# Two transformer blocks on one core: the second block's first modulation as row sums on VectorE

## What is computed

```python
def _modulation(cvec, w_ada, b_ada):
    m = jax.nn.silu(cvec) @ w_ada + b_ada
    return jnp.split(m, 3, axis=-1)
...
    sh, sc, gt = _modulation(c, w_ada, b_ada)
    sh_c, sc_c, gt_c = _modulation(c_ctx, w_ada, b_ada)
    h = _rms(x, norm_w) * (1.0 + sc[:, None, :]) + sh[:, None, :]
    hc = _rms(xc, norm_w) * (1.0 + sc_c) + sh_c
...
def swiglu(x, w1, w3, w2):
    return (jax.nn.silu(x @ w1) * (x @ w3)) @ w2
```

## Time and profile before

| | |
|---|---|
| time of three runs | 1367.22 us median, 1361.17 to 1367.77 |
| span of the profiled execution | 1363.3 us (its own time is not given) |
| TensorE busy | 1344.2 us, 99% |
| VectorE busy | 790.6 us, 58% |
| ScalarE busy | 640.8 us, 47% |
| granted TensorE clock | full in all 40 slices |
| DMA | 215.43 MB, 158 GB/s over the span |

### The profile page before, as it was taken

How to read it: one execution, slowest core, us unless ns; L and a number is a source line. 1 busy time by engine, 2 the same in 40 slices (tenths; PEclk the granted TensorE clock), 3 DMA queues, 4 the chain that set the end, 5 groups by cost and what they waited for, 6 DMA issues and landing times.

```text
span 1363.3 us, 24540 instructions
## 1 busy us (share of the span) xinstructions
PE 1344.2 (99%) x10306; PEld 1200.5 (88%) x10306; DVE 790.6 (58%) x1239; ACT 640.8 (47%) x1126; POOL 160.1 (12%) x131
## 2 busy tenths in 40 slices
PE   9999999999999999999999999999999999999999
PEld 8989999999855899999987777888888888879999
DVE  6976666557767666655724567433333455775554
ACT  6645444444365554455433445323232345555442
POOL 0020111001300012110004000111011100301110
PEclk9999999999999999999999999999999999999999
DMA  8535767556597455665432210222222234414553
GB/s 319 186 124 185 229 226 256 188 186 217 186 336 267 150 190 191 199 197 173 140 115 94 93 56 32 93 93 93 93 93 95 92 122 144 147 61 153 194 186 124
DMA packets 60974, 215.43 MB, mean 158 GB/s; under 512 B 6720, under 2 KB 12736, under 8 KB 57408
## 3 DMA queue, kind: packets, MB, share of 16 engines
q1 hardware_dynamic: 56272, 206.59, 45.4%
q10 hardware_dynamic: 4592, 7.26, 1.5%
HBM read 208.59 MB, written 1.05 MB: 154 GB/s over the span
## 4 chain that ended last, share of the span: by engine, by line
PE 88%; DVE 7%; ACT 3%; issue 1%; DMA 1%; SPq 0%; POOL 0%; ACTq 0%; DVEq 0%; POOLq 0%
PE psum L329 24%; PE psum L330 23%; PE psum L331 23%; DVE WL L261 3%; PE psum L1246 3%; PE psum L1271 2%; PE psum L1409 2%; PE psum L326 1%; PE psum L327 1%; PE psum L328 1%; ACT WH L256 1%; PE psum L2714 1%; PE psum L1602 1%; DMA stage<-ab_in 1%; PE psum L1250 1%
## 5 line engine op out<-in xcount | busy, mean ns | idle before, releaser
L329 PE MATMUL psum<-XX,WH 128*128 128x256 f32 (+1 forms) x1912 | 584.7, 306 | 8.2 <-DVE WL L261 2.8
L331 PE MATMUL psum<-XX,WL 128*128 128x256 f32 (+1 forms) x1912 | 576.3, 301 | 0.0
L330 PE MATMUL psum<-XX,WH 128*128 128x256 f32 (+1 forms) x1912 | 576.3, 301 | 0.0
L261 DVE TENSOR_TENSOR WL<-stage,WH 128x1024 fp32r<-128x1024 f32 x332 | 397.1, 1236 | 254.9 <-ACT WH L256 254.7
L256 ACT ACTIVATE WH<-stage 128x1024 fp32r<-128x1024 f32 x332 | 333.4, 1052 | 330.1 <-PE psum L331 286.0
L329 PEld LDWEIGHTS psum<-XX,WH 128*128 128x128 f32 x1912 | 359.4, 188 | 39.7 <-issue 13.8
L331 PEld LDWEIGHTS psum<-XX,WL 128*128 128x128 f32 x1912 | 359.9, 188 | 15.9
L330 PEld LDWEIGHTS psum<-XX,WH 128*128 128x128 f32 x1912 | 358.8, 188 | 15.7 <-issue 0.5
L329 PE MATMUL psum<-hidden,WH 128*128 128x256 f32 x352 | 97.5, 277 | 0.0
L331 PE MATMUL psum<-hidden,WL 128*128 128x256 f32 x352 | 97.2, 276 | 0.0
L330 PE MATMUL psum<-hidden,WH 128*128 128x256 f32 x352 | 97.2, 276 | 0.0
(11 more groups left out here) (288 smaller groups left out, 1675.7 us busy)
## 6 DMA issues: line engine op xcount, KB each, us to landing
stage<-w SPq DMA_DIRECT2D x132, 512.0 KB, 4.6
stage<-merge SPq DMA_DIRECT2D x80, 512.0 KB, 4.5
ring<-ada SPq DMA_DIRECT2D x24, 1024.0 KB, 7.0
stage<-in SPq DMA_DIRECT2D x44, 512.0 KB, 4.5
stage<-ab_in SPq DMA_DIRECT2D x22, 512.0 KB, 5.8
stage<-nsa_in SPq DMA_DIRECT2D x20, 512.0 KB, 4.8
stage<-out SPq DMA_DIRECT2D x16, 512.0 KB, 4.2
stage<-ab_out SPq DMA_DIRECT2D x8, 512.0 KB, 4.7
```

Source lines behind the costliest of these rows:

```text
L261: e.tensor_tensor(lo, raw, hi.bitcast(F32), ALU.subtract).then_inc(s_lo, 1)
L329: e.matmul(dst, wh, xh, start=start, stop=False)
L330: e.matmul(dst, wh, xl, start=False, stop=False)
L331: return e.matmul(dst, wl, xh, start=False, stop=stop)
```

## The change

The first layer's modulation leaves TensorE. Its matrix is laid out transposed: 24 rows of 128 features, each feature in one partition with its 1024 weights along the row. `cvecs` holds both vectors, copied into every partition. ScalarE takes the SiLU of them once in each feed-forward layer. `modulation_row` multiplies a row of weights with each vector and sums along it, so two instructions give 128 features for both vectors. Fourteen rows stand in f0 (c = 1 to 10 and m = 1 to 4), ten in f1 (c = 1 to 10). Their weights take twelve ring slots, which SyncE loads between the stage loads. The second layer's twelve blocks stay in the attention, spread over its 27 steps. The diff, cut to its core:

```diff
--- before.py
+++ after.py
+        ROWS = list(range(1, 8)) + list(range(21, 26))
...
         def ring_load(e, rings, name, src):
             if n >= NSLOT:
-                e.wait_ge(*pe.of(f"ring{n - NSLOT}"))
+                e.wait_ge(*(ve if n - NSLOT in ROWS else pe).of(f"ring{n - NSLOT}"))
...
         def ring_take(e, rings, cols, shape, **dims):
+            while rings.n in ROWS:
+                rings.n += 1
...
@@ ffn_vector, up-projections
                 if c > 0:
                     low_next(e, flow)
+                    modulation_row(e, l, 14 * l + c - 1)
                 e.wait_ge(*pe.of(f"{p}.w3.{c}"))
@@ ffn_vector, down-projections
+                if l == 0 and 1 <= m <= 4:
+                    modulation_row(e, l, 9 + m)
                 e.wait_ge(*pe.of(f"{p}.w2.{m}"))
@@ ffn_scalar
                 if c == 0:
                     inverse_scalar(e, p)
+                    meet(e, *["hn"[l] + ".end"] * 4)
+                    e.dma_start(M.rows, A["cvecs"].rearrange("p (v n) -> p v n", v=2)).then_inc(s_rows, 16)
                 e.wait_ge(*ve.of(f"{p}.up.{c}"))
                 e.activation(F.sg[c % 3], F.sg[c % 3], ACT.Silu).then_inc(*ac.tick(f"{p}.silu{c}"))
+                if c == 0:
+                    e.wait_ge(s_rows, 16 + 16 * l)
+                    e.activation(M.rows, M.rows, ACT.Silu).then_inc(*ac.tick(f"m.rows{l}"))
@@ ffn_sync
             for c in range(22 + 11):
                 load_next(e, flow)
-                if c in (12, 16, 20):
-                    next(ahead, None)
+                if c in ((0, 1, 2, 9, 13, 17, 21, 25, 29, 31), (0, 1, 2, 9, 13))[l]:
+                    next(ahead)
@@ new
+        M.rows, M.spent = view(2048, 2048, **two), C("decay", 768, 1024)
+
+        def modulation_row(e, l, t):
+
+            n = ROWS[t // 2]
+            w = ring[:, n % NSLOT * SLOT + t % 2 * 1024:n % NSLOT * SLOT + t % 2 * 1024 + 1024]
+            e.wait_ge(*ac.of(f"m.rows{l}"))
+            e.wait_ge(s_slot[n % NSLOT], 16 * (n // NSLOT + 1))
+            for v in range(2):
+                if v == 0 and t > 0:
+                    e.wait_ge(*ve.of(f"m.row{t - 1}"))
+                e.scalar_tensor_tensor(out=(M.spent, w)[v], in0=w, scalar=1.0, in1=M.rows[:, v, :], op0=ALU.mult, op1=ALU.mult,
+                                       accum_out=MODS[0][:, t, v:v + 1]).then_inc(*ve.tick(f"m.row{t}"))
+            if t % 2 == 1:
+                ve.mark(f"ring{n}")
+            if t == 23:
+                modulation_ends(e, 0)
+
+        def modulation_ends(e, l):
+
+            bias, nw = [v.rearrange("p (m a) -> p m a", a=1).to_broadcast([128, n, 2])
+                        for v, n in ((P("b_ada", 24 * l, 24), 24), (P("norm_w2", 8 * l, 8), 8))]
+            e.wait_ge(*ve.now())
+            e.tensor_tensor(MODS[l], MODS[l], bias, ALU.add).then_inc(*ve.tick())
+            e.wait_ge(*ve.now())
+            e.scalar_tensor_tensor(out=MODS[l][:, 8:16, :], in0=MODS[l][:, 8:16, :], scalar=1.0, in1=nw, op0=ALU.add,
+                                   op1=ALU.mult).then_inc(*ve.tick(f"m.{l}"))
@@ modulation_tensor, _turns, _vector, _scalar
-            for c in range(24):
+            for c in range(12):
@@ nsa_tensor, nsa_vector, nsa_scalar
-            attend_tensor(e, "n", N.units, N.S, N.T, scores, values, beside, evenly(24, 24), last, turns)
+            attend_tensor(e, "n", N.units, N.S, N.T, scores, values, beside, evenly(24, 10), last, turns)
@@ nsa_ahead, final_ahead, nsa_sync
+            for j in range(7):
+                ring_load(e, rings, f"rows{j}", A["ada_0"][j])
+                yield
-            for name, src in (("cmp_1", A["cmp_1"]), ("ada0", A["ada"][0]), ("ada1", A["ada"][1])):
+            for name, src in (("cmp_1", A["cmp_1"]), ("ada0", A["ada_1"][0]), ("ada1", A["ada_1"][1])):
...
+        def final_ahead(e, rings):
+            for j in range(7, 12):
+                ring_load(e, rings, f"rows{j}", A["ada_0"][j])
+                yield
...
-            for c in range(2, 24):
-                ring_load(e, rings, f"ada{c}", A["ada"][c])
+            for c in range(2, 12):
+                ring_load(e, rings, f"ada{c}", A["ada_1"][c])
@@ the arrays
-    arr["ada"] = np.ascontiguousarray(I["w_ada_2"].reshape(2, 4, 2, 128, 3, 4, 256).transpose(0, 4, 1, 3, 5, 2, 6)).reshape(
-        24, 128, 2048)
+    arr["ada_0"] = np.ascontiguousarray(I["w_ada_2"][0].T.reshape(12, 2, 128, 1024).transpose(0, 2, 1, 3)).reshape(12, 128, 2048)
+    arr["ada_1"] = np.ascontiguousarray(I["w_ada_2"][1].reshape(4, 2, 128, 3, 4, 256).transpose(3, 0, 2, 4, 1, 5)).reshape(
+        12, 128, 2048)
+    arr["cvecs"] = np.ascontiguousarray(np.broadcast_to(np.concatenate([I["c_2"][0], I["c_ctx_2"]])[None], (128, 2048)))
```

More of the change, by code:

```diff
@@ L178, in build @@
         s_out = sem("out_landed")
+        s_rows = sem("vector_rows_landed")
         s_swap = {name: sem(f"swapped_{name}") for name in SWAPPED}
@@ L1181, in ffn_scalar @@
                     square_scalar(e, "fn", m)
+                    if m == 0:
+                        e.wait_ge(*ve.of("m.0"))
                     e.activation(SQ1[:, m, :], X[:, m, NOW], ACT.Square, scale=P("final_norm", m)).then_inc(
@@ L1200, in ffn_gpsimd, with ffn_sync @@
             gp.mark(f"{p}.end")
-        def ffn_sync(e, flow, l, ahead=()):
-            ahead = iter(ahead)
+        def ffn_sync(e, flow, l, ahead):
             for c in range(22 + 11):
                 load_next(e, flow)
-                if c in (12, 16, 20):
-                    next(ahead, None)
+                if c in ((0, 1, 2, 9, 13, 17, 21, 25, 29, 31), (0, 1, 2, 9, 13))[l]:
+                    next(ahead)
                 if l == 0 and c == 8:
@@ L1426, in modulation_vector @@
         def modulation_vector(e):
-            for c in range(24):
+            for c in range(12):
                 if c % 4 == 3:
                     u = c // 4
-                    l, m = u // 3, u % 3 * 8
-                    to = MODS[l][:, m:m + 8, :].rearrange("p (g j) v -> p j g v", j=2)
-                    bias = P("b_ada", 24 * l + m, 8).rearrange("p (g j a) -> p j g a", j=2, a=1).to_broadcast([128, 2, 4, 2])
+                    m = u * 8
+                    to = MODS[1][:, m:m + 8, :].rearrange("p (g j) v -> p j g v", j=2)
+                    bias = P("b_ada", 24 + m, 8).rearrange("p (g j a) -> p j g a", j=2, a=1).to_broadcast([128, 2, 4, 2])
                     e.wait_ge(*pe.of(f"m.v{u}"))
@@ L1436, in modulation_vector @@
                     banks.emptied(f"m.v{u}", ve)
-                    if u % 3 == 2:
-                        nw = P("norm_w2", 8 * l, 8).rearrange("p (m a) -> p m a", a=1).to_broadcast([128, 8, 2])
+                    if u == 2:
+                        nw = P("norm_w2", 8, 8).rearrange("p (m a) -> p m a", a=1).to_broadcast([128, 8, 2])
                         e.wait_ge(*ve.now())
-                        e.scalar_tensor_tensor(out=MODS[l][:, 8:16, :], in0=MODS[l][:, 8:16, :], scalar=1.0, in1=nw,
-                                               op0=ALU.add, op1=ALU.mult).then_inc(*ve.tick(f"m.{l}"))
+                        e.scalar_tensor_tensor(out=MODS[1][:, 8:16, :], in0=MODS[1][:, 8:16, :], scalar=1.0, in1=nw,
+                                               op0=ALU.add, op1=ALU.mult).then_inc(*ve.tick("m.1"))
                 yield
         def modulation_scalar(e):
-            for c in range(24):
+            for c in range(12):
                 if c % 4 == 3:
@@ L1732, in finish @@
                     banks.emptied(f"n.value{it}{t2}{f}", ve)
-            attend_vector(e, "n", N.units, N.S, N.T, finish, beside, evenly(24, 24), True)
+            attend_vector(e, "n", N.units, N.S, N.T, finish, beside, evenly(24, 10), True)
             residual_vector(e, flow, "n", "f1", "n.begun")
@@ L1790, in done @@
                     e.activation(N.part(XH, n), N.value(n), ACT.Copy).then_inc(*ac.tick(f"n.xh{n}"))
-            attend_scalar(e, "n", N.units, N.S, N.T, beside, evenly(24, 24), True, done)
+            attend_scalar(e, "n", N.units, N.S, N.T, beside, evenly(24, 10), True, done)
             residual_scalar(e, flow, "n", "f1", ((ve, 23),))
@@ L2950, in sync @@
             nsa_sync(e, flow, rings)
-            ffn_sync(e, flow, 1)
+            ffn_sync(e, flow, 1, final_ahead(e, rings))
             layer_sync(e, flow, rings, 0)
```

## The result

The changed kernel takes 1374.08 us (median of 9 runs), the kernel before 1366.79 beside it (9 runs). The ratio is 1.0078, with an interval of 1.0057 to 1.0098: some 11 us slower by the ratio, 7.3 by the medians, where 1366.4 and no measurable change was forecast. The profiled executions have spans of 1371.9 and 1363.3 us, 8.6 apart. Between these two it is the same, so their stages may be subtracted.

What follows compares the result with a forecast made beforehand. TensorE was taken to bound the kernel, at 88% of the chain. Attention -11.6, down-projections +3.2 and transfer waits +7.6 sum to -0.8 us on the median 1367.2, giving 1366.4; range 1358 to 1378, likeliest case 1361 to 1373.

Steps and rivals of the forecast that it cites:

- ScalarE's wait for the transfer: Both feed-forward stages: ScalarE stands until both vectors land, delaying w3's second high parts; +4.2 and +3.4, together 7.6 us.
- I take 7.0: Feed-forward stages: assumed landing time in us of the 1 MB transfer, between 5.3 and 9.0 seen for others.
- the prediction's own rule: First turns of both stages: landing time passes into the wait; 5.3 us takes 1.7 off each, 9.0 adds 2.0.
- Rival B: Feed-forward stages: ScalarE's wait for the transfer decides; landings of 11 us give +7.2, 1374 us; chance 0.15.
- The attention: Sparse attention: removing twelve modulation blocks and three transpose pairs saves 7.6 us in the second half, 4.0 in the first.
- a group lasts from 427.50 to 439.66, 12.16 us: Attention's second half: a group of three units falls from 12.16 to 10.25 us, saving 1.9 each, 7.6 for four.
- Down-projections: First layer, m = 1 to 4: rows ahead of the residual delay ScalarE's high parts; +3.2 us, 2.0 with rows of 2.4.
- Up-projections: Both feed-forward layers: a row brings VectorE to 9.65 of a 10.88 us turn, so it fits; 0 us.
- The bound of 4.0 us: Up-projections: row time on VectorE up to which the added row still fits in a turn.
- Rival C: VectorE's product with a sum runs at half pace, slowing up- and down-projections; +24 us, 1391 us; chance 0.1.

Runs made afterwards that it cites:

- experiment 2: Three variants of the changed kernel: ring loads at chunks 0, 3, 6; at 4, 5, 6; transfer and products cut to two columns: ratios 1.0075, 1.0092, 1.0013.
- experiment 3: Changed kernel plus 12 extra fp32 products on TensorE ahead of the second w3 chunk in both layers: ratio 1.0049.
- experiment 5: Changed kernel with the SiLU one turn later, and the attention's twelve modulation blocks multiplying 16 of 256 columns: ratio 0.9921.
- experiment 4: Changed kernel with the SiLU one turn later, and the first layer's down-projection row products behind the residual and its low part: ratio 0.9949, measured again 0.9925.
- experiment 7: Changed kernel with the SiLU one turn later, and GpSimd's gate multiplication over 2 of 256 columns: span 1361.8 us, first products 1.22 us.
- the kernel with the loads apart: Changed kernel with each layer's second and third ring loads issued at chunks 3 and 6, not 1 and 2: ratio 1.0075.
- the fastest version: Changed kernel with SiLU one turn later, down-projection rows behind the residual, and five extra products in the attention's step 1: ratio 0.9919, span 1350.1 us.

## Why the prediction was wrong, step by step

- **ScalarE's wait for the transfer**: the right place and mechanism, the term mis-sized. It had 4.2 + 3.4 = 7.6 and measured 7.6 + 7.15 = 14.8. Of the 7.2 missing, two steps. The first is "I take 7.0" for the landing. That is what it takes with no ring load near it (6.8 and 7.4, experiment 2), and there the holes are 3.7 and 3.6, near the 4.2 and 3.4 reckoned. With the three loads it was 8.4 and 9.3, for which the prediction's own rule gives 5.6 and 5.7 (measured 5.3 and 5.5). That is 3.3. The other 3.9 has no step at all in the prediction, which forecast the holes but put nothing behind them: the granted clock was at 0.50 there, and it costs about 1.8 us each (experiment 3). Nothing in the profile before could show it, since its clock is full everywhere and it has no hole of 5 us.
- **Rival B** named this wait, but put the point from which it decides at a landing of 11 us. With the clock's part it decided at 8.4 and 9.3.
- **The attention**: -11.6 forecast, -9.0 measured. The failed step is "a group lasts from 427.50 to 439.66, 12.16 us": that was one group, taken for all four. TensorE's timeline of the kernel before has the scores that open the two groups ahead of it at

```profile
406.82 1.13 PE L1246 MATMUL psum<-arena 64*128 64x256 f32 x8
...
417.12 1.14 PE L1246 MATMUL psum<-arena 64*128 64x256 f32 x8
```

so these took 10.3 and 10.4 us, the first with three modulation blocks in it like the one of 12.16. In the changed kernel a group, forecast at 10.25, is

```profile
431.57 1.13 PE L1260 MATMUL psum<-arena 64*128 64x256 f32 x8
...
441.20 1.13 PE L1260 MATMUL psum<-arena 64*128 64x256 f32 x8
```

9.63 us. The second half then gave -3.9 and not -7.6. The first half gave -5.0, a bit more than 4.0, in spite of its hole. That chains of VectorE and ScalarE and not TensorE set the pace once blocks are gone held in one group (experiment 5); for the whole attention it is not shown.
- **Down-projections**: +3.2 forecast, +1.5 measured. A row is 2.4 us, the lower bound, and the prediction gave 2.0 for it. The mechanism, ScalarE's wait for the residual, is shown by experiment 4.
- **Up-projections**: 0 forecast, 0 measured in ten of eleven turns, though a row takes 3.5 us there and not 2.8, since GpSimd's gate blocks its first product (experiment 7). The bound of 4.0 us was closer than thought.
- **Rival C** fell: 1.21 us for a product with its sum. The Trainium skill's statement on half throughput ("Vector Engine (DVE) Microarchitecture Reference", section 7) is not what these 48 products show.

With the measured values in the prediction's sum: -9.0 + 1.5 + 14.8 = +7.3, and 0.95 before the change and 0.4 in the rest make the 8.6. B's +7.2 agrees with it by luck: its 15.6 came from a landing of 11 us, and its -11.6 and +3.2 for the attention and the down-projections were both too large.

## What to carry to other kernels

A wait put on an engine's queue costs what is queued behind it: here the transfer, not the 24 added rows, decided between 0.8% slower and 0.3% faster, and one turn later it was free. Price a landing by what will be in flight when it is issued, and where a hole in TensorE of some us is forecast, look for a half-clock stretch behind it: here it added 1.6 to 2.3 us to holes of 5.3 and 5.5. When a stage has repeated groups, average several before calling one typical.

## What the runs showed beside this

TensorE has two paces at full granted clock. The up-projections take either 5.44 or 5.65 us for a chunk, constant through a stage, and which one differs between executions and stages without going with any edit. Windows of 20 us in f0, of the kernel with the loads apart and of the kernel before:

```profile
190.00:210.00 20.00, 20.00 (x172) 1.00 0.76 250
```

```profile
190.00:210.00 20.00, 20.00 (x179) 1.00 0.74 244
```

They hold 172 passes or 179, both at clock 1.00: 4%. (Other such windows had 172, 173, 178 or 179.) The kernel before and the changed one have the fast pace in both feed-forward stages and the slow one from 1260 to 1280; the fastest version has the fast pace in all three, and from f1's inverse root to the end it takes 870.3 us and not 873.9: some 3.5 of the 13 us between its span and that of before. At 4.6 us for the 22 chunks of one stage (I had expected 6 to 8 us for a stage) it is large enough for much of the spread between runs of one kernel (1360.1 to 1374.0 for the kernel before); that it is the cause was not tried, nor what sets it.
